# Rotary position embedding: partner rows fetched by small SBUF-to-SBUF transfers instead of by permutation products on TensorE

## What is computed

```python
def partial_rope(x, pos):
    half = ROT_DIM // 2                                  # 8
    inv = ROPE_THETA ** (-jnp.arange(half) * 2.0 / ROT_DIM)
    ang = pos[:, None] * inv[None, :]
    cos, sin = jnp.cos(ang)[None, :, None, :], jnp.sin(ang)[None, :, None, :]
    xr = x[..., :ROT_DIM]
    x1, x2 = xr[..., :half], xr[..., half:]
    rot = jnp.concatenate([x1 * cos - x2 * sin, x2 * cos + x1 * sin], axis=-1)
    return jnp.concatenate([rot, x[..., ROT_DIM:]], axis=-1)
...
        h = rms_norm(x, norm_mix_pre[l])
        z = h @ w_in[l]
        q = partial_rope(q, pos)
        k = partial_rope(k, pos)
        o_attn = sliding_window_gqa_sinks(q, k, v, sinks[l])
        o_ssm = s5_mixer(u, lam_re[l], lam_im[l], log_dt[l], b_re[l], b_im[l], c_re[l], c_im[l], d_skip[l], w_glu[l])
        mixed = (g_attn * (o_attn @ w_branch[l][:Q_W]) + g_ssm * (o_ssm @ w_branch[l][Q_W:])) @ w_out[l]
```

## Time and profile before

| | us |
|---|---|
| median of the runs (lowest to highest) | 2595.93 (2595.38 to 2596.93) |
| the profiled execution | 2594.04 |
| its span | 2592.4 |
| PE busy | 2508.3 (97%) |
| DVE busy | 1350.9 (52%) |
| ACT busy | 690.5 (27%) |
| POOL busy | 218.9 (8%) |

### The profile page before, as it was taken

How to read it: one execution, slowest core, us unless ns; L and a number is a source line. 1 busy time by engine, 2 the same in 40 slices (tenths; PEclk the granted TensorE clock), 3 DMA queues, 4 the chain that set the end, 5 groups by cost and what they waited for, 6 DMA issues and landing times.

```text
span 2592.4 us, 30238 instructions
## 1 busy us (share of the span) xinstructions
PE 2508.3 (97%) x11543; PEld 2037.6 (79%) x11543; DVE 1350.9 (52%) x1597; ACT 690.5 (27%) x858; POOL 218.9 (8%) x319
## 2 busy tenths in 40 slices
PE   8989999999999999979999999999999999999994
PEld 6766788888788888857888888888888888888883
DVE  8857488888434443357433444344434443444347
ACT  5226332323322222234221222122212221222121
POOL 1130234340000000011000000000000000000002
PEclk9999999999999999989999999999999999999997
DMA  5451345453334453223333323222232233223341
GB/s 203 104 174 45 94 138 167 130 167 122 130 97 134 145 189 108 94 97 101 98 98 98 97 97 97 97 97 93 94 104 97 89 97 105 97 89 97 105 146 65
DMA packets 85349, 291.47 MB, mean 112 GB/s; under 512 B 11264, under 2 KB 11312, under 8 KB 85280
## 3 DMA queue, kind: packets, MB, share of 16 engines
q1 hardware_dynamic: 63936, 232.81, 27.6%
q0 software_dynamic: 9408, 32.50, 3.9%
q10 hardware_dynamic: 11936, 25.22, 3.1%
HBM read 261.06 MB, written 23.13 MB: 110 GB/s over the span
## 4 chain that ended last, share of the span: by engine, by line
PE 90%; DVE 6%; DMA 2%; ACT 1%; issue 1%; POOL 1%; ACTq 0%; DVEq 0%; POOLq 0%
PE main L1442 29%; PE main L1444 29%; PE main L1443 29%; DMA b_scratch<-b_even_lo 1%; DVE mlp_acc L1419 1%; PE side L1507 1%; PE side L1496 1%; DMA coef_by_channel<-coef_scratch 1%; DVE w_lo L790 1%; PE side L1517 1%; PE side L1578 1%; DMA x<-x_t 1%; DVE softmax_max L1024 0%; DVE square_sum L814 0%; DVE mixed L1310 0%
## 5 line engine op out<-in xcount | busy, mean ns | idle before, releaser
L790 DVE TENSOR_TENSOR w_lo<-w_raw,w_hi 128x1024 fp32r<-128x1024 f32 x436 | 542.0, 1254 | 354.8 <-ACT w_hi L469 329.4
L469 ACT ACTIVATE w_hi<-w_raw 128x1024 fp32r<-128x1024 f32 x436 | 451.8, 1055 | 918.4 <-PE main L1444 890.5
L1442 PE MATMUL main<-m_hi,w_hi 128*128 128x512 f32 x1280 | 501.4, 392 | 20.0 <-POOL m_lo L446 19.9
L1443 PE MATMUL main<-m_lo,w_hi 128*128 128x512 f32 x1280 | 500.8, 391 | 0.0
L1444 PE MATMUL main<-m_hi,w_lo 128*128 128x512 f32 x1280 | 500.4, 391 | 0.0
L1442 PE MATMUL main<-a_hi,w_hi 128*128 128x512 f32 x1024 | 398.3, 389 | 0.0
L1443 PE MATMUL main<-a_lo,w_hi 128*128 128x512 f32 x1024 | 398.3, 389 | 0.0
L1444 PE MATMUL main<-a_hi,w_lo 128*128 128x512 f32 x1024 | 398.3, 389 | 0.0
L1442 PE MATMUL main<-h_hi,w_hi 128*128 128x512 f32 x800 | 321.6, 402 | 13.3 <-DVE h_lo L808 8.6
L1444 PE MATMUL main<-h_hi,w_lo 128*128 128x512 f32 x800 | 313.9, 392 | 0.0
L1443 PE MATMUL main<-h_lo,w_hi 128*128 128x512 f32 x800 | 313.4, 392 | 0.0
(11 more groups left out here) (279 smaller groups left out, 2030.4 us busy)
## 6 DMA issues: line engine op xcount, KB each, us to landing
w_raw<-wstream SPq DMA_DIRECT2D x436, 512.0 KB, 3.5
gate_scratch<-gate_stage ACTq DMA_DIRECT2D x16, 512.0 KB, 3.3
b_weights<-b_scratch ACTq DMA_DIRECT2D x32, 192.0 KB, 3.8
u_rows<-u_hi_lo ACTq DMA_DIRECT2D x96, 64.0 KB, 3.7
x<-x_t POOLq DMA_DIRECT2D x8, 512.0 KB, 6.1
gate_attn<-gate_scratch POOLq DMA_DIRECT2D x8, 512.0 KB, 3.7
gate_ssm<-gate_scratch POOLq DMA_DIRECT2D x8, 512.0 KB, 4.4
x<-x_t POOLq DMA_DIRECT2D x4, 1024.0 KB, 9.1
```

The source lines that it names most:

```text
L469: nc.scalar.activation(WH[:, s], RAW[:, s], ACT.Copy).then_inc(hi_ready, 1)
L790: tt(WL[:, s], RAW[:, s], WH[:, s].bitcast(F32), ALU.subtract).then_inc(lo_ready, 1)
L1442: mm(o, wh, xh[:, k0 + k], start=first and k == 0, stop=False)
L1443: mm(o, wh, xl[:, k0 + k], start=False, stop=False)
```

## The change

The permutation products on PE go, with the PERM matrix. POOL clears a new tile `swapped` (two buffers of two tiles of 512 columns) when the squares of x are summed, because the tile lies where `x_squares` did. After each `bank_read` of a query block it issues four transfers that copy 8 partitions each, of two tiles (32 KB), from the query tile into `swapped`, with the halves exchanged; for the key tile the four are 16 KB each. DVE multiplies `swapped` in place by the sine table, whose sign now carries the minus of the first half, multiplies the query by the cosine and adds. In POOL's stream swaps 0, 1 and 2 stand ahead of the wait for `rows_ready`, swap 3 behind the coefficient loads and swap 4 behind the 24 stores of `b_scratch`. `rope_k` no longer waits for the transposed values.

```diff
@@ tiles
+    SWP = at("swapped", [2, 2, T], 160)
-    PERM = at("perm", [P], 201.5)
@@ gpsimd
             pool.dma_start(ROPE[:], consts[:, 0:2 * T].rearrange("p (a t) -> p a t", a=2)).then_inc(consts_landed, 16)
-            pool.dma_start(PERM[:], consts[:, 1024:1152]).then_inc(consts_landed, 16)
...
+            pool.wait_ge(xsum_step, 4)
+            nc.gpsimd.memset(SWP[:], 0.0).then_inc(swap_cleared, 1)
+            pool.wait_ge(swap_cleared, 1)
+
+            def swap(b):
+                pool.wait_ge(bank_read, b + 1)
+                if b >= 2:
+                    pool.wait_ge(rope_free, b)
+                to, x = (SWP[:, b % 2], Q[:, 2 * b:2 * b + 2]) if b < 4 else (SWP[:, 0, 0], KV[:, 0])
+                half = ROT // 2
+                for h in (0, HEAD):
+                    pool.dma_start(to[h:h + half], x[h + half:h + ROT]).then_inc(swap_landed[b % 2], 16)
+                    pool.dma_start(to[h + half:h + ROT], x[h:h + half]).then_inc(swap_landed[b % 2], 16)
+
+            for b in range(3):
+                swap(b)
             pool.wait_ge(rows_ready, 1)
             pool.dma_start(coef_dram..., CT4[:]).then_inc(coef_stored, 16)
...
+            swap(3)
             for r, (parts, turn) in enumerate((((BBH, BBL), 1), ((B1H, B1L), 2))):
                 pool.wait_ge(bl_ready, turn)
...
+            swap(4)
@@ vector
             def rope_q(b):
-                xx, t, psum, cos_, sin_ = rope(Q[:, 2 * b:2 * b + 2], b)
-                link(tt(t, psum, sin_, ALU.mult))
-                link(tt(xx, xx, cos_, ALU.mult))
-                link_to(tt(xx, xx, t, ALU.add), rope_free, b + 2)
+                x, t = Q[:, 2 * b:2 * b + 2], SWP[:, b % 2]
+                v.wait_ge(consts_landed, 48)
+                v.wait_ge(swap_landed[b % 2], 64 * (b // 2 + 1))
+                tt(t, t, both(ROPE[:, 1]), ALU.mult)
+                link(tt(x, x, both(ROPE[:, 0]), ALU.mult))
+                link_to(tt(x, x, t, ALU.add), rope_free, b + 2)
 
             def rope_k():
-                v.wait_ge(rope_mm, 5)
-                v.wait_ge(vt_done, 1)
+                v.wait_ge(swap_landed[0], 64 * 3)
                 v.wait_ge(pads_set, 1)
-                link(tt(KV[:, 1], side[:, 0], ROPE[:, 1], ALU.mult))
+                t = SWP[:, 0, 0]
+                tt(t, t, ROPE[:, 1], ALU.mult)
                 link(tt(KV[:, 0], KV[:, 0], ROPE[:, 0], ALU.mult))
-                link_to(tt(KTOK[:, P:P + T], KV[:, 0], KV[:, 1], ALU.add), rope_free, 6)
+                link_to(tt(KTOK[:, P:P + T], KV[:, 0], t, ALU.add), rope_free, 6)
@@ tensor
-            def rope(x, b, tiles):
-                pe.wait_ge(bank_read, b + 1)
-                pe.wait_ge(rope_free, b + 1)
-                for t in range(tiles):
-                    ins = mm(side[:, t], PERM[:], x(t), start=True, stop=True)
-                ins.then_inc(rope_mm, 1)
...
-                    if j in (1, 5):
-                        h = j // 4
-                        if i == 0 and j == 1:
-                            pe.wait_ge(consts_landed, 64)
-                        rope(lambda t: Q[:, i * 4 + (2 * h + t)], i * 2 + h, 2)
...
                 if n == 21:
-                    rope(lambda t: KV[:, 0], 4, 1)
+                    pe.wait_ge(bank_read, 5)
```

## The result

The changed kernel takes 2603.93 us (median of 8, 2603.03 to 2605.08) against 2595.9 before (median of 8, 2594.11 to 2596.93): ratio 1.0032, 95% interval 1.0021 to 1.0042. It is 8.0 us slower. The forecast was 2599.5, range 2593 to 2609; the sign that it gave as likeliest, no change within 0.2%, was not the one that came.

A forecast was written before the change was run, and what follows sets the result against it. The prediction took the chain of coefficient loads and `b_scratch` stores, up to the first mask, as the bound, not PE's products. 0 + 0 + 1.5 - 2 + 0.7 + 4.5 - 1.1 = +3.6 us gave 2599.5, range 2593 to 2609.

The forecast's parts named there:

- Where the end is set: First score tile's mask on DVE: the kernel's end moves with this mask, at 166.04 us before.
- the signs that were named: Timeline checks: store at 91 on POOL, gap before unit 12 about 5.9 us, mask 4 to 5 us later.
- first rival: Coefficient store on POOL: coefficients late in full, 7.1 us in place of 1.5, total near 2606; chance 0.27.
- The removed products at 0: PE's permutation products: 6.0 us of work, each ahead of a wait whose end is set elsewhere; worth 0.
- Swap 0: First query rotation on DVE: transfers land near 50.6, hidden by 0.9 us; 0, bounds 0 to 1.2.
- Swap 2: POOL ahead of the coefficient store: store 7.1 us later, `b_bar` only +1.5 us late, bounds -1.5 to +7.1.
- The relief of the stores: Stores of `b_scratch`: loads of weight units 28 and 29 out of their way; -2 us, bounds -4 to 0.
- Swap 4 behind the stores: Key tile's swap on POOL: lands 0.7 us after the last `b_scratch` store, bounds 0.3 to 3.
- The order term: DVE behind swap 4: `rope_k` and `w_lo` of units 24 and 25 now follow the stores; +4.5 us.
- second rival: Key tile's swap overtakes the stores, landing near 147; `rope_k` stays hidden, total 2597.4; chance 0.15.
- The clock: PE around the first mask: most slow-clock time falls where PE waits anyway; -1.1 us, bounds -1.7 to 0.
- The sum: All terms together: +3.6 us, bounds -2.4 to +15.8; 2599.5 against the median.

The follow-up runs named there:

- before_no_mm: Kernel before with its nine permutation products left out and nothing in their place, so the rotation is not computed; 2593.2 us beside 2596.27, ratio 0.9988.
- before_wait3: Kernel before with one wait added: POOL waits for the third query block ahead of `rows_ready`, no transfers issued there; 2595.86 us beside 2596.12.
- swap4_act: Changed kernel with only the key tile's swap moved from POOL to ACT's queue, after ACT's rounding of unit 22; 2600.09 us, ratio 1.0013 to before.
- after_ropek25: Changed kernel with `rope_k` moved on DVE from unit 23 to unit 25, behind `w_lo` of units 24 and 25; 2603.48 us, ratio 1.0031 to before.
- reorder: Changed kernel: swaps 2, 3 behind POOL's coefficient loads, swap 4 on ACT after unit 23, rotations of query pairs 2, 3 at units 20, 22; 2591.32 us.
- swap2_act: Changed kernel with only swap 2 moved from POOL to ACT's queue, after ACT's rounding of unit 15; 2603.16 us, ratio 1.0024 to before.
- after_hold16: Changed kernel with one DVE wait added: `w_lo` of unit 16 not begun before the coefficients landed; 2602.59 us, ratio 1.0030 to before.
- before_swap2: Kernel before with swap 2's clearing, wait and four transfers added on POOL ahead of the coefficient store, result unused; 2599.4 us, ratio 1.0011.
- before_turn10: Kernel before with only PE's transposition of the coefficients moved, after unit 10 in place of unit 11; 2595.2 us beside 2596.12, ratio 0.9996.

## Why the prediction came out as it did, by its steps

**Where the end is set.** Right. The shift of the first mask is what arrives at the end, less the clock: 9.5 us at the mask, 7.8 at the gate, 8.0 in the medians. Of the signs that were named, the forecast's came for the store on POOL, `rope_k` and PE's idle time before unit 24, but so did the first rival's, `b_bar` over 3 us late, and the mask was 9.5 us late where 4 to 5 was said.

**The removed products at 0.** Right in the main, bound by before_no_mm to 0.6 by its profile and 3.1 (0.8 to 5.5) by its medians, out of 6.0. The foretold gap of 5.9 us before unit 12 came as three, 6.15 together.

**Swap 0.** Right: no wait at `rope_q(0)`; after it was issued at 48.38 on POOL the rotation began at 52.50, with no idle time before it.

**Swap 2, the step that failed.** The term was +1.5 and it measured +5.9. The rule behind it, that loads and weight units trade places in full engines and the total is the same, held for what it was argued from: the wait alone moves the store by 5 us and costs nothing. What the sum left out is what the four transfers do. They stand before the store in the queue (2 us), its return grows from 2.12 to 4.94 us with the engines busy where they had been idle (3.99 with the wait alone), and the loads then run at 92 to 98 GB/s where before_wait3 has 135 to 141. DVE, freed from waiting for PE's product, also issues the load of unit 20 in their midst, which goes with a part of it. Why the loads run slower stays open. The first rival's price, 7.1 us, was near in size by luck: the loads were issued not 7.1 but 9.6 us later and then took 3.7 us less, and lateness of the store by itself was free.

**The relief of the stores.** -2 foretold, -2.4 measured. The reason given, that the loads of units 28 and 29 are out of the way, is shown only in part: the stores took 36.7 us in swap4_act and 35.7 in after_ropek25, which have these loads among them, but 34.1 in reorder, which has them too.

**Swap 4 behind the stores.** Its landing 0.7 us after them was foretold and 0.7 measured. The order term, what DVE has to do between swap 4 and the mask beyond what it had before, was +4.5 and measured +5.2: the `w_lo` pair of 2.36 us took 2.64 and the single one, which took 1.26 before, 1.63. POOL, which starts its rotation work at the end of the stores, ran beside them, but it did so in the kernel before as well, so that it is the cause isn't shown. Nor was PE hidden with room to spare, as the prediction had it. The first score tile of after stands so in PE's time line:

```profile
175.23 1.23 PE L1506 MATMUL side<-k_t,q 64*128 64x256 f32 x4
```

It ends at 176.46 and `w_lo` at 176.39, and the mask begins at 176.51: two paths of one length, and in after_ropek25 PE's was the longer. swap4_act shows the swap overtaking on another queue; on POOL's own it landed behind the stores, and the second rival had no ground.

**The clock.** -1.1 foretold, -1.7 measured, if all that is shorter from the mask to the gate is put down to it. Busy time by stretches after, columns as in rows 8:

```profile
170.00:176.00 6.00, 3.60 (x10) 2.33 (x10) 5.90 (x6) 0.00 (x0) 5.69 (x8) 0.50 0.41 115
176.00:178.00 2.00, 2.00 (x10) 1.24 (x6) 1.09 (x2) 0.00 (x0) 1.92 (x3) 0.80 0.76 238
```

The granted clock is 0.50 (1.2 GHz) from 170 to 176, around PE's idle time of 6.33 us, and 0.80 from 176 to 178. So nearly all of the slow time lies ahead of the mask at 176.51, and little of it behind: 2 x 0.20 = 0.4 us lost at most, against 1.7 before. So the rows account for about 1.3 of the 1.7. The prediction took the slow time ahead of the mask as free. That was only just so: PE's path to the first score tile ran at 0.50 and came out as long as DVE's.

**The sum.** 5.9 - 2.4 + 0.7 + 5.2 - 1.7 = +7.7, against +3.6 foretold. Of the 4.1 us between, 4.4 are swap 2, 0.7 the order term, and -1.0 the two that helped more. The range held because the full lateness was in it. The chances were too kind to "within 0.2%": a term with bounds of -1.5 and +7.1 had been placed near its low end by one argument. The range's high end is said to take in the late coefficients with all else as summed, 2608.5; that sum gives 2605.1 (2595.9 + 3.6 + 5.6), and the 2608.5 does not come out of the terms.

## What to carry to other kernels

A small transfer costs what its queue and the instruction stream behind its wait hold, and not its bytes: 16 KB took 19 us to land behind 24 stores, and the three instructions that waited for it and the two behind them put 5.2 us onto the path. Before work is taken off the busiest engine, name the wait that comes next on it; if that wait ends elsewhere, the work is free to keep, and moving it onto a queue that feeds the real chain is a loss. And once it is moved, place it by urgency: the same transfers and rotations in another order were some 12 us faster than the change, and 4.8 (2.3 to 7.0) faster than the kernel before.

## What the runs showed of the hardware that was not expected

- A queue of its own carried a 4 x 16 KB swap past the stores: DVE had it 8.1 us after the last of its issues began (swap4_act, 150.32 to 158.44). But a 4 x 32 KB swap issued on the same queue among the eight broadcast loads took 14.0 us, counted in the same way (swap2_act). The Trainium skill, page "DMA: Bandwidth & Descriptors", section "Issuing engines are not separate DMA queues", says that DMAs of all engines run on the same 16 DMA engines and interleave; both runs agree, and they show that how soon a transfer gets through differs by what is in flight or by its size, which were not told apart.
- Issuing such a transfer held ACT for 0.63 to 1.24 us each in swap2_act and 1.25 to 2.20 us in swap4_act, with the DMA engines at a share of 0.84 to 1.18, against 0.50 to 0.54 us on POOL in after.
- Eight loads of 128 KB ran at 135 to 141 GB/s (before_wait3), at 113 (after_hold16) or at 90 to 98 (before_swap2, after), with the share of the engines at 1.0 or more in all and no weights in flight. What decides between them was not found.
- After the same stop of PE before unit 12 (3.24 us before, 3.26 in before_wait3, 3.22 in before_turn10) the granted clock stayed at 1.00 in the first and fell to 0.5 (1.2 GHz) in the other two, in one profile each. The rotation that waits for PE's product began 1.6 and 2.7 us later there.
